# One load sent ahead of a weight piece, casts taken out of the head of ScalarE's loop, one idle matmul less, in a fused decoder block on one core

## The reference

```python
h = rms_norm(x, g_mix)                       # x: (256, 1024)
q, k, v, cb, cc, cx, ga, gc = split(h @ w_in + b_in)     # w_in: 1024 x 6656
y_attn = sliding_window_attention(rope(q), rope(k), v, sinks) @ w_attn_o
y_conv = (cb * causal_short_conv(cc * cx, w_conv)) @ w_conv_o
merged = sigmoid(ga) * y_attn + sigmoid(gc) * y_conv
x = x + merged @ w_out
h = rms_norm(x, g_ffn)
logits = h @ w_router + b_router             # 32 experts, the top 4 by token, softmax over them
x = x + sum of top_w[e] * ((g * sigmoid(1.702 g) * (u + 1)) @ w_down[e] + b_down[e])
        # g, u: clamped h @ w_gate[e] + b_gate[e] and h @ w_up[e] + b_up[e]
return rms_norm(x, g_final)
```

## Time and profile before

| | |
|---|---|
| median of three runs | 1192.78 us (1192.71 to 1193.74) |
| the profiled execution, its own time | 1192.05 us |
| its span | 1190.2 us |
| TensorE busy | 1119.3 us (94%) |
| VectorE, ScalarE, GpSimd busy | 364.4, 212.5, 128.2 us |
| DMA moved | 448.06 MB, mean 376 GB/s |
| DMA in forty slices | 143 to 245 GB/s in the second to eighth, 426 to 430 in nearly all from the eleventh |

### The profile page before, as it was taken

How to read it: one execution, slowest core, us unless ns; L and a number is a source line. 1 busy time by engine, 2 the same in 40 slices (tenths; PEclk the granted TensorE clock), 3 DMA queues, 4 the chain that set the end, 5 groups by cost and what they waited for, 6 DMA issues and landing times.

```text
span 1190.2 us, 18119 instructions
## 1 busy us (share of the span) xinstructions
PE 1119.3 (94%) x7454; PEld 572.4 (48%) x7454; DVE 364.4 (31%) x653; ACT 212.5 (18%) x393; POOL 128.2 (11%) x98
## 2 busy tenths in 40 slices
PE   8899999999999999999999999999999999999996
PEld 7899999984343333333333333333333333333342
DVE  6966785673111122111111111111111111111121
ACT  5566655451000000000000000000000000000001
POOL 4453444430000000000000000000000000000000
PEclk9999999999999999999999999999999999999999
DMA  8444666799999999999999999999999999999995
GB/s 283 143 154 157 220 201 217 245 399 413 427 428 426 428 428 428 428 428 428 428 428 428 428 428 427 428 426 428 428 428 428 430 428 428 429 429 428 427 426 218
DMA packets 71834, 448.06 MB, mean 376 GB/s; under 512 B 5497, under 2 KB 45781, under 8 KB 46709
## 3 DMA queue, kind: packets, MB, share of 16 engines
q1 hardware_dynamic: 71328, 446.75, 91.2%
q10 hardware_dynamic: 469, 0.77, 0.2%
HBM read 446.06 MB, written 1.05 MB: 376 GB/s over the span
## 4 chain that ended last, share of the span: by engine, by line
PE 48%; DMA 45%; DVE 3%; issue 2%; ACT 1%; SPq 0%; DVEq 0%; ACTq 0%
PE psum L686 26%; DMA ring<-in_w_up 23%; DMA ring<-in_w_gate 17%; PE psum L465 9%; PE psum L469 4%; DMA ring<-in_w_down 3%; PE psum L699 2%; PE psum L651 2%; DMA ring<-in_w_out 1%; PE psum L712 1%; DMA ring<-in_w_in 1%; ACT work L1016 1%; DVE w L1107 1%; PE psum L666 1%; PE psum L482 0%
## 5 line engine op out<-in xcount | busy, mean ns | idle before, releaser
L686 PE MATMUL psum<-ring,work 128*64 128x512 f32 x3072 | 686.3, 595 | 50.7 <-DMA ring<-in_w_gate 28.9
L686 PEld LDWEIGHTS psum<-ring,work 128*64 128x64 f32 x3072 | 212.4, 137 | 473.8 <-issue 363.1
L1343 DVE TENSOR_SCALAR work<-psum 128x512 f32<-128x512 f32 x32 | 22.1, 692 | 417.4 <-PE psum L686 417.4
L1476 POOL TENSOR_TENSOR w<-ring,w 128x1024 fp32r<-128x1024 f32 x38 | 100.7, 2657 | 108.0 <-ACT w L873 105.5
L1514 POOL COPY chosen<-pick 96x64 bf16 (+1 forms) x32 | 7.5, 234 | 868.8 <-PE psum L712 868.8
L465 PE MATMUL psum<-hL,w 128*128 128x256 f32 x384 | 95.3, 286 | 1.1 <-ACT w L873 0.6
L465 PE MATMUL psum<-hH,w 128*128 128x256 f32 x384 | 94.1, 283 | 0.0
L1107 DVE TENSOR_TENSOR w<-ring,w 128x1024 fp32r<-128x1024 f32 x38 | 80.1, 2112 | 37.7 <-ACT w L873 37.7
L1348 DVE TENSOR_SCALAR work<-psum 128x512 f32<-128x512 f32 x32 | 22.1, 692 | 192.8 <-PE psum L686 192.8
L873 ACT CAST w<-ring 128x1024 fp32r<-128x1024 f32 x74 | 74.4, 1048 | 27.8 <-PE psum L469 20.2
L465 PEld LDWEIGHTS psum<-hL,w 128*128 128x128 f32 x384 | 73.6, 192 | 4.0 <-issue 2.2
(11 more groups left out here) (202 smaller groups left out, 833.4 us busy)
## 6 DMA issues: line engine op xcount, KB each, us to landing
ring<-in_w_gate SPq DMA_DIRECT2D x64, 2048.0 KB, 38.1
ring<-in_w_up SPq DMA_DIRECT2D x63, 2048.0 KB, 39.7
ring<-in_w_down SPq DMA_DIRECT2D x61, 2048.0 KB, 39.3
ring<-in_w_in SPq DMA_DIRECT2D x26, 1024.0 KB, 5.0
ring<-in_w_down SPq DMA_DIRECT2D x6, 1024.0 KB, 37.6
ring<-in_w_conv_o SPq DMA_DIRECT2D x4, 1024.0 KB, 5.0
ring<-in_w_attn_o SPq DMA_DIRECT2D x4, 1024.0 KB, 5.2
ring<-in_w_out SPq DMA_DIRECT2D x4, 1024.0 KB, 6.2
```

What stands on the lines that cost most here:

```text
L686: mm = pe.matmul(psum[64 * h:64 * h + 64, b, :], src[:, k, :], w[:, k2, h * 512:(h + 1) * 512], start=(bias_of is None and k == 0), stop=( ...
L1343: v.tensor_scalar(gm, psum[:, 4, :], LIMIT, None, ALU.min).then_inc(gmin_ready, 1)
L1476: g.tensor_tensor(wL[:, par, 0, :, :], slot(s).rearrange("p (k n) -> p k n", k=KB)[:, :, 0:P], wH[:, par, 0, :, :].bitcast(F32), ALU.subtr ...
```

## The change

In SP's list of the last pieces the load of run (0, 2), with the wait for piece 32's matmuls, stands ahead of the third w_out piece (n = 36) where it stood ahead of the fourth (n = 37). On ScalarE the cast of each turn's c = 1 piece leaves the head of the loop: that of turn 0 (piece 3) stands ahead of the loop and of the four K copies, and each turn ends with the cast of what was the next turn's first (c = 7, which is the next turn's c = 1); the last turn so casts piece 27, and the list behind the loop starts a piece later. And of two idle matmuls in the router's chain one is left.

```diff
             for nth, src in enumerate(tail):
-                if n == NP1 - 1:
+                if n == NP1 - 2:
                     sp.wait_ge(blocks_done, 2 * (NIN + 2 * NKV - 1))
                     load_run(0, 2, 2)
+                if n == NP1 - 1:
                     sp.wait_ge(blocks_done, 2 * (NIN + 2 * NKV))
                     load_run(0, 3, 3)
...
-            for n in range(KEEP_WARM):
-                pe.matmul(bank(2), ident, cst[:, 0:512], start=True, stop=True)
+            pe.matmul(bank(2), ident, cst[:, 0:512], start=True, stop=True)
             pe.wait_ge(M_ready, 1)
...
+            split_high(3, 0, 16 * 2, 1)
             act_e.wait_ge(kz_ready, 1)
             act_e.wait_ge(rotated, 1)
             for odd in range(2):
...
             with act_e.Fori(0, NKV) as i:
-                split_high_in_turn(i, 1)
                 act_e.wait_ge(blocks_done, i * 12 + 6)
                 act_e.wait_ge(rotated, i + 1)
...
                 act_e.wait_ge(u_ready, i + 1)
+                split_high_in_turn(i, 7)
 
             for n in range(NIN, NIN + 2 * NKV):
...
-                if n + 1 < NP1:
+                if n > NIN:
                     split_high(n + 1, (n + 1) % RING1, 16 * ((n + 1) // RING1 + 1), (n + 1) % 2)
```

## The result

| | before | after |
|---|---|---|
| median of four runs | 1193.03 us | 1206.72 us (1204.91 to 1208.33) |
| the profiled execution | 1192.05 us | 1205.2 us |
| its span | 1190.2 us | 1203.4 us |
| TensorE busy | 1119.3 us (94%) | 1122.8 us (93%) |

The ratio is 1.0113, with an interval of 1.0101 to 1.0125: **13.7 us slower**, where 7 were forecast. The sign and the collision came out; the time lies above the range (1202.6).

The account below looks back on a forecast made before the run. Bound taken: TensorE until about 240 us, then a DMA stream of fixed bytes and rate. 1192.05 + 8.7 - 1.6 = 1199.15 us for the profiled execution; the median stands 0.73 higher, 1199.9 us; range 1194.3 to 1202.6.

Parts of the forecast that it names:

- The collision: First stage, each turn: VectorE's and GpSimd's subtractions exclude one another; GpSimd goes first, moving VectorE's chain by 3.55 us.
- The table load behind the wait: ScalarE, each turn: the 1.28 us table load starts only when TensorE ends the q piece, delaying the q copy.
- Rival (1): ScalarE's table load runs ahead of the wait, gaining 5.27 + 1.6 us: 1185.9, chance 0.08.
- The two L1107 passed: VectorE's two L1107 subtractions each let a GpSimd one go first; the second ends at 90.1 instead of 86.54.
- Rivals (2) and (3): (2) no collision, 0.68 us lost a turn: 1188.6, chance 0.06; (3) one L1107 passed: 1194.3, chance 0.06.
- TensorE stands 3.49 us in each turn: First stage: TensorE waits 3.49 us for the late L1202 before its transposes (L564) in every turn.
- Turn 0 was to gain 1.78: First stage, turn 0: earlier casts less the stand put L564 at 58.40 against 60.18, 1.78 us gained.
- 8.7 us longer: First stage's sum: 1.78 us gained in turn 0, 3 x 3.49 = 10.47 lost in turns 1 to 3.
- 1.6 us gained: Tail: moving run (0, 2) lands the last w_out piece earlier and the stream keeps 1.6 us, bounds 0 and 2.0.
- Run (0, 3) with the bias copies lands at 244.3: Load step in the tail: the fourth w_out piece follows at 247.3 instead of 248.95, 1.65 us earlier.
- I cost it at nothing: Router's chain: one idle matmul fewer brings the ranks 0.6 us earlier, with no effect on the time.
- Rival (4): The collision comes, and the clock or a late w_out piece takes the tail's 1.6 us: 1201.5, chance 0.15.

Follow-up runs that it names:

- GpSimd held back: Changed kernel, table load still late, with GpSimd's cut of each turn's c = 3 piece waiting for VectorE's of c = 2: 1187.76 us, ratio 0.9958.
- 1024 columns: Kernel before with one 1024-column activation on ScalarE ahead of the q copy in each turn: 1207.67 us, ratio 1.0123.
- idle matmuls in the stand: Changed kernel with three idle matmuls on TensorE in the stand before each turn's transposes: 1201.11 us, ratio 1.0061.
- the table load ahead: Changed kernel with a one-column activation at ScalarE's loop head, drawing the table load ahead of the wait for the q piece: 1188.39 us, ratio 0.9967.
- the casts alone: Kernel before with only the change's moved ScalarE casts, old place of the load and both idle matmuls: 1208.08 us, ratio 1.0130.
- the load alone: Kernel before with only run (0, 2) moved ahead of the third w_out piece: 1193.14 us, ratio 1.0000.
- the bias copies alone: Kernel before with only the third group of bias copies sent a piece earlier, right behind the second: 1193.16 us, ratio 1.0000.
- these with the load: Kernel before with the third group of bias copies sent a piece earlier and run (0, 2) moved as in the change: 1193.39 us, ratio 1.0003.
- 320 columns: Kernel before with one 320-column activation on ScalarE ahead of the q copy in each turn: 1194.54 us, ratio 1.0009.

## Why the prediction was right, and where it was wrong

- **The table load behind the wait: right.** 1.28 us right ahead of L912 in each turn, behind idleness ended by TensorE; no sign of a drain of another 1.38 us. Rival (1), 1185.9, is out.
- **The two L1107 passed: right**, shown by the timelines, by the order alone (GpSimd held back) and by the delay alone (1024 columns). In its turn the first L1108 is in line at 14.18 us, before at 12.91: 1.27 later, where 1.28 was forecast. Rivals (2) and (3) are out.
- **"TensorE stands 3.49 us in each turn": right**, 3.45 measured. Turn 0 was to gain 1.78 and gained 1.96, or 1.75 without the 0.21 by which the profile was ahead. The condition that the collision comes in turn 0 too held: its stand is 2.96.
- **The sum of the first stage, "8.7 us longer": wrong**, 12.7 measured. The missing term is the clock behind the stands, 3 x 1.44 = 4.3 us. I had looked at the granted clock only in the router's chain, and priced a stand as its own length; that is the step that failed. The matmuls that followed each stand ran at 1.2 GHz; with idle matmuls in the stand they did not, and the part behind the transposes was back at 8.91. The Trainium skill ("TensorE: Matmul & The Clock Gate", Part 1) has the half clock as the default that sustained activity releases; I had weighed that against one idle matmul, and not against the four stands that the same text forecast. The rows agree with it behind three of after's four.
- **"1.6 us gained" by the load: wrong**, nothing measured (1.0000), and in after 0.5 lost behind piece 34. The step that failed is "Run (0, 3) with the bias copies lands at 244.3": I gave the small copies the stream's rate and SP no time, but they held SP for 4.9 us behind the two loads; and I had missed ScalarE's wait for them. The third piece itself landed at 240.3 and not at 238.6. With the bias copies sent early the fourth cast came 1.35 earlier, near the forecast, and the time did not move; so the second half of the step, that the stream keeps it, isn't shown either, and the cause stays open.
- **"I cost it at nothing", the idle matmul: wrong by about 1.2 us when it is alone** (1.0001 to 1.0020). The one profile fits the mechanism that the text named as the danger (half clock for 7.3 us, the tenth run sent later), but it isn't certain to come: of the five profiles with one idle matmul, two show some 7 us of half clock there (this one, and the one with idle matmuls in the stand), two none (the table load ahead, GpSimd held back), and in after the clock fell for 3.3 us from 278.3 on, in the pause ahead of the ranks; there the price can't be told apart: the casts alone were no faster than the whole change.
- **The balance for the profiled execution:** forecast 1199.15, measured 1205.2; 4.0 of the 6.05 are the first stage (12.7 against 8.7), 2.1 the tail (0.5 lost against 1.6 gained). The medians differ by 0.8 more, since the profiled run was one of after's two short ones. By the 0.5's own uncertainty (above) the tail's share says only that the 1.6 did not come. Rival (4) had the clock or a late piece taking the tail's 1.6 us; it put the clock in the router, and it fell in the turns.

## What to carry to other kernels

Where a forecast makes TensorE stand for some microseconds among dense matmuls, price what the matmuls behind the stand lose to the clock as well as the stand: here a stand of 3.45 cost 4.9 wherever the clock fell behind it. When two engines exclude one another, read who is in line first and by how much; a table load that moves by a microsecond can swap them, and then a wait of the unhurried engine for the hurried one is the cheap cure. And a small transfer behind large ones holds its queue and whoever waits for it: count the queue's time, not the bytes.

## What the runs showed that I had not expected

- **The clock does not fall behind every stand.** After a stand of 2.96 us in turn 0 it stayed at 2.4 GHz in after and fell in the run of the casts alone. TensorE stood for 2.17 us until 42.52 before, at 2.4 GHz behind it; in the profile of the load alone it stood for 2.16 until 42.35, and the clock was down behind it, but up in the router's chain at 263.3 to 266.6, where before it was down. The profiles of the bias copies alone, of these with the load, and of the 320 columns go with the load alone (0.50 at 43.6 to 46.2, 1.00 at 262 to 268). Which it is differs from execution to execution, and no run here says by what. The windows of the load alone:

```profile
43.00:46.70 3.70, 3.70 (x22) 3.04 (x19) 3.70 (x3) 0.00 (x0) 3.70 (x2) 0.57 0.54 174
263.30:266.60 3.30, 2.59 (x11) 0.82 (x10) 2.63 (x14) 2.23 (x3) 1.08 (x1) 1.00 0.92 377
```

- **After and the casts alone spread more** (3.4 and 2.5 us over four runs) than before (1.0 over four, 2.4 over the 21 beside the last runs); that fits the first point. After's two short executions (1204.91 and 1205.2) have a mean granted clock of 0.993, its two long ones (1208.23 and 1208.33) of 0.990: by an estimate from these numbers, 0.003 of 1206 us is 3.6 us of full speed, which is some 7 us more at 1.2 GHz, or two stretches of 3.3.
- **Four copies of 32 KB held the issuing queue for 4.9 us** behind 3 MB of loads, 2.6 us behind 1 MB (before: 605 to 612 ns apiece), and 605 to 610 ns apiece at 224.5 to 227.1 us with the order mended. Behind the 3 MB the first took 2.5 us, the second 1.0 and the other two 0.61 each.
